# The recurrent mixer of a four-layer stack: order of the ScalarE and VectorE instructions around the gates

## The reference

```
def odd_mixer(xn, w_in, w_out, conv_w, conv_b, w_r, b_r, w_i, b_i, lam):
    z = (xn @ w_in).astype(jnp.float32)
    h = rglru_mixer(z[..., :LRU_WIDTH], conv_w, conv_b, w_r, b_r, w_i, b_i, lam)
    y = (h * jax.nn.gelu(z[..., LRU_WIDTH:])).astype(w_out.dtype)
    return (y @ w_out).astype(xn.dtype)
# rglru_mixer: xc = causal convolution of width 4 plus bias
    gate_r = sigmoid(einsum(xh, w_r) + b_r);  gate_i = sigmoid(einsum(xh, w_i) + b_i)   # 4 blocks of 256
    log_a = -RG_C * gate_r * softplus(-lam);  a = exp(log_a);  mult = sqrt(-expm1(2.0 * log_a))
    h[t] = a[t] * h[t-1] + mult[t] * (gate_i[t] * xc[t])
```

## Time and profile before

| | |
|---|---|
| median of 3 runs | 1277.36 us (1277.1 to 1277.82) |
| the profiled execution | 1277.36 us; its span, first to last instruction, 1275.6 us |
| PE busy | 1247.0 us, 98% |
| PEld, DVE, ACT, POOL busy | 81%, 64%, 52%, 7% |
| mean granted TensorE clock | 0.998 of full speed |
| the mixer's stretch, od0 to the end of od_out | about 327.4 to 437.3 us |
| DMA, mean | 170 GB/s |

### The profile page before, as it was taken

One profiled execution on the slowest core, in us unless ns is written; L12 is line 12 of the kernel. 1 busy time (PEld: TensorE's weight loads), 2 busy tenths in 40 slices (PEclk: granted clock), 3 DMA queues, 4 the chain that ended last, 5 costly groups with the idle time before them and its releaser, 6 DMA issues.

```text
span 1275.6 us, 15785 instructions
## 1 busy us (share of the span) xinstructions
PE 1247.0 (98%) x6366; PEld 1031.6 (81%) x6366; DVE 815.3 (64%) x1048; ACT 669.7 (52%) x975; POOL 91.3 (7%) x113
## 2 busy tenths in 40 slices
PE   6999999999999999999999999999999999999998
PEld 4877888888887888888888888888888888888886
DVE  7986766654787765564687656565546784665552
ACT  7666544433788554443587635444336653544431
POOL 2410100000110000000123100000000300000000
PEclk9999999999999999999999999999999999999999
DMA  7224465545644565545555224555455323555551
GB/s 298 100 84 143 171 212 184 193 171 198 215 165 165 182 208 188 192 172 198 171 198 192 73 75 161 212 180 198 166 197 177 132 100 132 198 178 185 195 173 62
DMA packets 32392, 216.60 MB, mean 170 GB/s; under 512 B 3888, under 2 KB 4272, under 8 KB 7232
## 3 DMA queue, kind: packets, MB, share of 16 engines
q1 hardware_dynamic: 30240, 210.19, 47.7%
q0 software_dynamic: 1360, 4.78, 1.2%
q10 hardware_dynamic: 720, 0.63, 0.1%
HBM read 214.54 MB, written 1.05 MB: 169 GB/s over the span
## 4 chain that ended last, share of the span: by engine, by line
PE 81%; DVE 10%; ACT 5%; issue 3%; DMA 1%; POOL 1%; SPq 0%; DVEq 0%; ACTq 0%
PE PS L451 22%; PE PS L453 22%; PE PS L452 22%; PE PS L457 4%; DVE WL L1655 3%; PE PS L488 2%; PE PS L491 2%; PE PS L489 2%; PE PS L723 2%; ACT WH L1059 2%; PE PS L747 1%; ACT HTh L1076 1%; DVE YG L1932 1%; DMA RAW<-in_w 1%; DVE st L1792 0%
## 5 line engine op out<-in xcount | busy, mean ns | idle before, releaser
L1655 DVE TENSOR_TENSOR WL<-RAW,WH 128x2048 fp32r<-128x2048 f32 (+2 forms) x200 | 443.9, 2222 | 327.9 <-ACT WH L1059 327.8
L1059 ACT ACTIVATE WH<-RAW 128x2048 fp32r<-128x2048 f32 (+2 forms) x200 | 371.7, 1862 | 381.1 <-PE PS L453 380.1
L451 PE MATMUL PS<-WH,HTh 128*128 128x512 f32 (+1 forms) x848 | 335.0, 395 | 1.9 <-DVE WL L1655 1.9
L453 PE MATMUL PS<-WH,HTl 128*128 128x512 f32 (+1 forms) x848 | 329.0, 388 | 0.0
L452 PE MATMUL PS<-WL,HTh 128*128 128x512 f32 (+1 forms) x848 | 328.4, 387 | 0.0
L451 PEld LDWEIGHTS PS<-WH,HTh 128*128 128x128 f32 x848 | 159.5, 188 | 34.4 <-DVE WL L1655 3.2
L453 PEld LDWEIGHTS PS<-WH,HTl 128*128 128x128 f32 x848 | 159.2, 188 | 33.3
L452 PEld LDWEIGHTS PS<-WL,HTh 128*128 128x128 f32 x848 | 159.6, 188 | 30.5
L451 PE MATMUL PS<-WH,YAh 128*128 128x512 f32 x402 | 158.9, 395 | 2.6 <-DVE YAl L1671 2.2
L453 PE MATMUL PS<-WH,YAl 128*128 128x512 f32 x402 | 156.7, 390 | 0.0
L452 PE MATMUL PS<-WL,YAh 128*128 128x512 f32 x402 | 156.5, 389 | 0.0
(11 more groups left out here) (364 smaller groups left out, 1488.8 us busy)
## 6 DMA issues: line engine op xcount, KB each, us to landing
RAW<-in_w SPq DMA_DIRECT2D x196, 1024.0 KB, 4.9
BC<-in_rows POOLq DMA_DIRECT2D x4, 512.0 KB, 3.9
YG<-in_mem POOLq DMA_DIRECT2D x4, 512.0 KB, 4.8
X<-in_x SPq DMA_DIRECT2D x2, 512.0 KB, 6.4
RAW<-in_w SPq DMA_DIRECT2D x4, 256.0 KB, 5.8
BC<-in_s SPq DMA_DIRECT2D x1, 512.0 KB, 11.0
BB<-in_s SPq DMA_DIRECT2D x1, 512.0 KB, 11.5
YG<-in_s SPq DMA_DIRECT2D x1, 512.0 KB, 12.3
```

The source lines that it names most:

```text
L451: e.matmul(out, ah, bh, start=start, stop=False)
L453: return e.matmul(out, al, bh, start=False, stop=stop)
L1059: e.activation(WH[:, c % NW, w], RAW[:, c % NR, w], ACT.Copy).then_inc(S.hi, 1)
L1655: e.tensor_tensor(WL[:, c % NW, w], RAW[:, c % NR, w], WH[:, c % NW, w].bitcast(f32), SUB).then_inc(S.lo, 1)
```

## The change

The same instructions are issued; the order on ScalarE and on VectorE changes, that on TensorE, GpSimd and SyncE does not.

```
 # ScalarE
             e.wait_ge(S.lamd, 1)
+            gates_tanh(0, G0, (0, 1))
             conv_parts(1)
-            gates_tanh(0, G0, (0, 1, 2, 3))
+            gates_tanh(0, G0, (2, 3))
...
             gates_decay(1)
-            gates_square(0)
-            gates_square(1)
             e.wait_ge(S.used, PLAN["mem01"][1] + 1)
             mem_v(0, (2, 3))
             feed(PLAN["mem01"][1])
+            gates_square(0)
+            gates_square(1)
+            feed(PLAN["od2"][0])
+            gain_turn("memk0", lambda j: KM[0][:, j:j + 2, :], col("memk_norm_2", 0), (4, 5))
             gates_root(0)
             gates_root(1)
-            feed(PLAN["od2"][0])
-            gain_turn("memk0", lambda j: KM[0][:, j:j + 2, :], col("memk_norm_2", 0), (4, 5))
...
-            def last_heads():
-                od_turn(3)
-                gates_out((2, 3))
-
-            wide_mm(PLAN["od_out"], 3, last_heads)
+            wide_mm(PLAN["od_out"], 3, lambda: od_turn(3), (lambda: gates_out((2, 3)),))
 # VectorE
             conv(3)
+            feed(PLAN["mem00"][1])
             conv_lo(1)
-            feed(PLAN["mem00"][1])
...
             gates_in(1)
+            feed(PLAN["mem01"][1])
             gates_root(0)
             gates_root(1)
-            feed(PLAN["mem01"][1])
             feed(PLAN["od2"][0])
...
             gates_out((0, 1))
+            feed(PLAN["od3"][0])
             gates_lo((0, 1))
-            feed(PLAN["od3"][0])
             feed(PLAN["od3"][1])
-            wide_mm(PLAN["od_out"], 3, last_heads)
+            wide_mm(PLAN["od_out"], 3, after=(last_heads,))
```

## The result

The changed kernel takes 1284.28 us (median of 6, 1283.51 to 1287.55) against 1277.79 (median of 6, 1277.1 to 1279.49) for the one before on the same chip: ratio 1.0053, 95% interval 1.004 to 1.0065. That is 5.1 to 8.3 us slower, 6.8 by the ratio. The forecast was 4.4 us and its range ended 6.0 above the profiled run. Direction, places and waits were right; 2.4 us are missing in it.

The account below looks back on a forecast made before the run. TensorE's matmuls and its waits bound the kernel. Od_out late 2.71, third chunk's wait 1.64 and 0.08 for a slower second matmul give 4.43 us: 1277.36 + 4.43 = 1281.8 us, 0.35% slower, range 1279.7 to 1283.4.

Parts of the forecast that it names:

- TensorE's two waits: Late starts ahead of gates(1), 0.76 us, and od_out, 1.34 us: the reordering can win 2.10 us at most.
- the one called "issue": The 0.76 us late start ahead of gates(1); its 0.60 us idle was claimed to be waiting for conv_lo(1).
- parts 1 to 4: Tanh before conv_parts(1); ScalarE order up to roots; split before first gates_lo; split before last_heads: 4.43 us together.
- part 3: VectorE split ahead of the first gates_lo, 2.2 us; od_out 2.71 us late, including part 1's 1.43.
- I take nothing for both waits of over 2 us, as after the 1.18 us of idle: Waits ahead of gates(1) and od_out: no clock loss added, since matmuls kept their pace behind 1.18 us of idle.
- a granted clock under 1.00 in the stretch: Sign in the changed kernel's trace that would show the forecast wrong.
- The slow stretch of the earlier trace: From 31.50 on in the kernel before: clock 0.54 for 3.5 us after little TensorE work, costing 1.6 us.
- the other bound: Upper price of a clock fall behind a long TensorE wait: 1.6 us, kept only for the range.
- The rival that named this: The clock falls after one of the waits, adding 1.6 us: 1283.4 us, 8% chance.
- the about 1.1 that I worked out: Part 2: ScalarE's split for od2's second chunk, waiting for TensorE, starts at 384.30 instead of 383.17.
- the rival of 2%: The table load ahead of the roots stops ScalarE for longer, od_out 0.9 us later: 1282.7 us, 2% chance.

Follow-up runs that it names:

- the last experiment: Kernel before, with conv_parts(1) ahead of the key squares and gates_out, gates_lo of heads 0 and 1 ahead of later scans: 1276.34 us, ratio 0.9986.
- Each part alone: Four runs, each putting one of the change's four reorderings alone into the kernel before: ratios 1.0010, 0.9995, 1.0027 and 1.0013, in order.
- The fillers: Changed kernel with 17, 10 and 6 throw-away matmuls ahead of gates(1), od_out and its third chunk: 1282.94 us, ratio 1.0032 to the kernel before.
- the control with fillers: Kernel before with 4 throw-away matmuls ahead of gates(1) and 4 ahead of od_out: 1278.66 us, ratio 1.0004.

## Why the prediction was wrong

**Right: what bounds, and that little could be won.** TensorE's two waits were the whole reserve, 2.10 us; the last experiment took 1.96 of them. That the one called "issue" is the wait for `conv_lo(1)` is shown by the same run: ScalarE's copy came earlier there, and the step ahead of `gates(1)` was 0.38 us instead of 0.88.

**Right: parts 1 to 4 with a full clock.** Their sum 4.43 is 4.40 where the clock is held up. In that run, counted from the start of the mixer, `gates(1)` is 1.42 us later than before (forecast 1.43), the roots 5.5 (5.4), the scans 0.55 (0.45), od_out 2.70 (2.71) and its third chunk 4.27 (4.35). Each part alone is within 0.15 us of what was expected for it from the same rows, with the 2.8 us of part 3's fall taken off.

**Wrong: the price of a wait beyond the wait itself.** The step is "I take nothing for both waits of over 2 us, as after the 1.18 us of idle". That row was the wrong one to go by. The runs show about 1.55 us in each fall behind a wait: behind the 2.52 us ahead of od_out in 4 of 4 traces, ahead of `gates(1)` behind 2.06 us in 3 of 5 and behind 2.22 us in the one trace that has it. The fillers took both falls away. The forecast named "a granted clock under 1.00 in the stretch" as a sign that it was wrong, and that sign came.

The trace of before had a row nearer in length. The slow stretch of the earlier trace rows stands behind one idle of 2.92 us, with full matmuls ahead of it and transposes behind:

```profile
31.23 0.33 PE L457 MATMUL PS<-ident,Qn 128*128 128x128 f32 x1 [2.92 <-ACT Qn L1076]
```

That is 0.4 us from the 2.52 ahead of od_out, and the 1.18 is 1.3 us from it. Had I taken the other bound, 1.6 us from the earlier trace rows, for both, the forecast would have been 1285.0 with 1283.4 for one fall; the measured 6.8 us over is what 4.4 and one and a half falls give. The rival that named this had 8% and only one fall in its price, and the range ended with it. The Trainium skill ("TensorE: Matmul & The Clock Gate", Why this matters for your kernels) warns against idle gaps between bursts of matmuls, but its table means gaps longer than both of these. The falls here came behind shorter ones, 2.06 and 2.52 us, so the measurement goes beyond the page's warning.

**The shift runs through the chain.** A fall behind `gates(1)` also moves everything that waits for TensorE: ScalarE was idle for 1.77 + 0.64 us ahead of the splits at 381.96 and 387.43. With the clock held up it was 0.27 + 0.64, near the about 1.1 that I worked out. The roots came 7.0 us later than before instead of the 5.5 with the clock held up, and od_out 4.3 instead of 2.7. So the fall is passed on in full, as the mixer's 7.5 = 4.4 + 2 x 1.55 also shows: the scans waited for the roots, and the roots stood behind ScalarE's waits for TensorE.

**Right: the table load.** In the changed kernel it is 1.28 us (402.50) and the root starts 0.02 behind its end; the rival of 2% didn't happen.

**Open.** Why the clock falls behind the same 2.06 us in one execution and not in another is not settled by these runs. Nor is how often, in executions without a profile. The length of the idle alone does not decide it: in the first layer the clock fell behind 0.83 us of idle in 6 of 14 traces, and in this mixer it never fell behind 1.48 us.

## What to carry to other kernels

When TensorE is the bound, an idle gap costs its own length and may cost the half clock behind it: price each wait that a change makes longer with both, and keep both ends in the range once for each such wait. Look through the whole trace for a gap near in length, and not only for one near in place. An instruction moved ahead of the one that TensorE waits for can be paid almost in full, however idle its engine is on average: the split of part 3 took 2.2 us and cost 1.9. Where a gap can't be avoided, throw-away matmuls into a free PSUM bank held the clock up here, and they tell a clock effect from others; comparing the length of one stage, not the whole run, showed differences of tenths of a microsecond.

## What the runs showed of the hardware

- Idle of TensorE in this mixer and the clock behind it, by traces: 3.16 us, fall in 1 of 1, with a spell of 6.08 us at 0.51; 2.52 us, fall in 4 of 4; 2.22 us, 1 of 1; 2.06 us, 3 of 5; 1.48 us, none in 7; 1.18 us and less, none.
- In the first layer, whose instructions are the same in all these kernels, the clock fell behind 2.91 to 2.97 us of idle in 11 of 14 traces; in the other three, the changed kernel's first among them, it stayed at 1.00. Behind 0.83 us of idle, which follows a series of short matmuls of 64 columns, it fell in 6 of 14. These six enter the mixer at 328.5 to 329.6 us, the other eight at 327.3 to 328.1.
- In some traces the fall doesn't come at once: the first matmuls behind the 2.52 us still come at full pace, and the slow steps begin up to 1.0 us later. That is why the stretches that start at such a wait show 0.60 and 0.61.
- The loss of a fall, by mixer lengths less the sums at full clock: 6.10, 5.98 and 6.14 less 4.43, 4.01 less 2.4, and, for two falls each, half of (7.52 less 4.43) and half of (7.63 less 4.43): 1.5 to 1.7 us, alike for matmuls of 256 and of 512 columns. The fall behind 3.16 us of idle took 2.8.
- The spread of the kernel before (1276.9 to 1280.3 over all its runs) may have the same source. Its one trace has no fall behind the 0.83 us; that of the control with fillers, whose mixer has the same length, has one and took 1278.9.
